# Attention in a fused encoder block: each transposition of probabilities as two halves of 64 queries

## What is computed

```
x = x + 1/2 * SwiGLU_1(RMSNorm(x))
h = RMSNorm(x);  q_r,k_r,v_r,g_r, q_a,k_a,v_a, gate_r,gate_a = h @ W_in
A: retention, 4 heads, both directions      B: windowed attention, see below
x = x + W_out( sigmoid(gate_r) * A + sigmoid(gate_a) * B )
x = x + 1/2 * SwiGLU_2(RMSNorm(x));  y = RMSNorm(x)
```

```
m = max(max(sc), sink);  p = exp(sc - m);  p = p / (sum(p) + exp(sink - m));  o = p @ v
```

## Time and profile before

| | us |
|---|---|
| median of 3 runs (2065.56 to 2068.51) | 2066.97 |
| the profiled execution | 2067.74 |
| its span in the trace | 2065.9 |
| TensorE busy, share of the span | 98% |
| VectorE, ScalarE, GpSimd | 64%, 35%, 44% |

### The profile page before, as it was taken

One profiled execution on the slowest core, in us unless ns is written; L12 is line 12 of the kernel. 1 busy time (PEld: TensorE's weight loads), 2 busy tenths in 40 slices (PEclk: granted clock), 3 DMA queues, 4 the chain that ended last, 5 costly groups with the idle time before them and its releaser, 6 DMA issues. The chain is left out here.

```text
span 2065.9 us, 25975 instructions
## 1 busy us (share of the span) xinstructions
PE 2018.8 (98%) x9240; PEld 1646.5 (80%) x9240; DVE 1328.3 (64%) x1478; ACT 731.6 (35%) x975; POOL 900.3 (44%) x564
## 2 busy tenths in 40 slices
PE   8999999999999999999999999999999999989997
PEld 7888888877877888888876668888888888877876
DVE  7766666677776525525676665467766666677765
ACT  5433333343333321222224554325333333343332
POOL 0244344478996312212122212252334334479992
PEclk8999999999999999999999999999999999999998
DMA  3232333366352211111211124331423323383532
GB/s 136 87 122 90 103 112 106 117 218 209 123 173 97 87 62 43 59 61 41 92 41 62 43 91 137 144 134 62 133 97 100 108 96 121 110 283 130 192 97 82
DMA packets 106865, 227.29 MB, mean 110 GB/s; under 512 B 9392, under 2 KB 30000, under 8 KB 106800
## 3 DMA queue, kind: packets, MB, share of 16 engines
q1 hardware_dynamic: 75680, 175.14, 24.9%
q10 hardware_dynamic: 31120, 51.29, 7.1%
HBM read 165.05 MB, written 61.34 MB: 110 GB/s over the span
## 5 line engine op out<-in xcount | busy, mean ns | idle before, releaser
L2042 POOL TENSOR_TENSOR w_lo<-stage,w_hi 128x1024 fp32r<-128x1024 f32 x54 | 143.0, 2649 | 437.2 <-ACT w_hi L1001 437.2
L1619 DVE SCALAR_TENSOR_TENSOR x<-ps,x 128x512 f32<-128x512 f32 x280 | 187.3, 685 | 106.4 <-PE ps L669 103.9
L600 PE MATMUL ps<-a_hi,w_hi 128*128 128x512 f32 x752 | 250.3, 400 | 1.1 <-DVE q_a L1810 0.6
L600 PE MATMUL ps<-a_lo,w_hi 128*128 128x512 f32 x752 | 242.9, 391 | 0.0
L600 PE MATMUL ps<-a_hi,w_lo 128*128 128x512 f32 x752 | 242.8, 391 | 0.0
L2057 POOL TENSOR_TENSOR gb<-gb,rstd 128x512 f32<-128x512 f32 x42 | 92.4, 2201 | 323.6 <-DVE gb L1551 301.9
L600 PEld LDWEIGHTS ps<-a_hi,w_hi 128*128 128x128 f32 x752 | 140.3, 188 | 37.4 <-issue 10.9
L600 PEld LDWEIGHTS ps<-a_hi,w_lo 128*128 128x128 f32 x752 | 141.5, 188 | 29.9
L600 PEld LDWEIGHTS ps<-a_lo,w_hi 128*128 128x128 f32 x752 | 141.8, 189 | 27.4
L669 PE MATMUL ps<-t_hi,hi 128*128 128x512 f32 x352 | 139.1, 395 | 13.0 <-DVE x L1619 8.1
L669 PE MATMUL ps<-t_lo,hi 128*128 128x512 f32 x352 | 137.3, 390 | 0.0
(11 more groups left out here) (309 smaller groups left out, 4606.9 us busy)
## 6 DMA issues: line engine op xcount, KB each, us to landing
stage<-wstream SPq DMA_DIRECT2D x56, 512.0 KB, 3.5
b_spill<-diff SPq DMA_DIRECT2D x88, 256.0 KB, 3.7
st_a<-win SPq DMA_DIRECT2D x42, 512.0 KB, 3.4
st_b<-win SPq DMA_DIRECT2D x42, 512.0 KB, 4.0
t_lo<-b_spill SPq DMA_DIRECT2D x40, 512.0 KB, 7.5
b_spill<-rawv SPq DMA_DIRECT2D x66, 256.0 KB, 4.0
a_lo<-b_spill SPq DMA_DIRECT2D x30, 512.0 KB, 5.1
x<-xT SPq DMA_DIRECT2D x16, 512.0 KB, 6.5
```

Source lines behind the costliest of these rows:

```text
L600: mm = pe.matmul(ps[:, bank, :], w[0:r, k, :], mv[0:r, k, HALF * half:HALF * half + HALF], start=first and part == 0, stop=final and part ...
L1619: dve.scalar_tensor_tensor(out=x[:, m, part], in0=ps[:, bank, :], scalar=0.5, in1=x[:, m, part], op0=ALU.mult, op1=ALU.add).then_inc(xacc, 1)
L2042: pool.tensor_tensor(w_lo[:, parity, :, :], stage[:, parity, :, :], f32(w_hi[:, parity, :, :]), ALU.subtract).then_inc(wlo_done, 1)
```

## The change

Each 128x128 transposition becomes two of 64 queries x 128 keys. The half with queries 0 to 63 lies in rows 0 to 63 of the array and goes to bank 6; the half with queries 64 to 127 lies in rows 64 to 127 and goes to bank 7. One `turn_p` so fills half of both banks, and every `turn_p` waits for the copy of the one directly before it. In the gate units the three calls of each half move from after k-steps 1, 2, 3 to after 1, 3, 5, and from after 0, 1, 2 to after 0, 2, 4. ScalarE's copy reads 256 numbers of each of two banks and puts the halves of each head together again.

```diff
                 else:
-                    pe.wait_ge(pT_done, 6 * i + (idx - 1 + SEED))
+                    pe.wait_ge(pT_done, 6 * i + (idx + SEED))
                 for a in range(GRP):
-                    mm = pe.transpose(ps[:, 6 + idx % 2, P * a:P * a + P], pr[kv][:, a, P * j:P * j + P], ident)
+                    for u in range(2):
+                        rows = slice(64 * u, 64 * u + 64)
+                        mm = pe.transpose(ps[:, 6 + u, 64 * a:64 * a + 64], pr[kv][rows, a, P * j:P * j + P], ident[rows, rows])
                 mm.then_inc(p_turned, 1)
...
-                    if before is not None and 1 <= k <= 3:
-                        turn_p(before, 1, k - 1)
+                    if before is not None and k in (1, 3, 5):
+                        turn_p(before, 1, k // 2)
...
-                      between=lambda k: turn_p(i, 0, k) if k <= 2 else None).then_inc(unit_done, 1)
+                      between=lambda k: turn_p(i, 0, k // 2) if k in (0, 2, 4) else None).then_inc(unit_done, 1)
...
-                    act.activation(pT[kv][:, j, :], ps[:, 6 + (3 * kv + j) % 2, :], ACT.Copy).then_inc(pT_done, 1)
+                    act.activation(pT[kv][:, j, :].rearrange("p (a u n) -> p u a n", a=GRP, u=2),
+                                   ps[:, 6:8, 0:256].rearrange("p u (a n) -> p u a n", a=GRP), ACT.Copy).then_inc(pT_done, 1)
```

## The result

The change made the kernel slower by 0.75%: 2084.01 us in the median of 4 runs (2082.22 to 2085.49) against 2066.26 (2062.97 to 2068.51), ratio 1.0075 with a 95% interval of 1.0058 to 1.0092. Forecast were 2080.4 and a ratio of 2080.4/2066.97 = 1.0065. The profiled execution has a span of 2080.8 us against 2065.9.

The account below looks back on a forecast made before the run. TensorE, busy 98% of the span and all of an attention block, was taken as the bound. Turns 6.3, score waits 6.0 and the tail after block 7 1.1 sum to 13.4 us, giving a median of 2080.4, range 2077 to 2085.

Parts of the forecast that it names:

- TensorE's stream decides: Attention block: TensorE is busy in all 19.75 us, so a longer turn_p lengthens the kernel.
- A turn costs 0.58 in place of 0.44: Each turn_p on TensorE: +0.14 us, 6.3 us over the 45 turns inside gate halves.
- the gap of 0.32: Entry of a turn: from last gate matmul to first half's load, 0.32 where 0.23 is seamless, costing 0.09 us.
- the exposed load: First weight load of a turn's halves, not hidden behind other work: 0.058 us.
- steps of 0.06: Inside a turn: row halves run side by side, leaving four steps of 0.058, together 0.23 us.
- the exit: From a turn back to gate matmuls: change of shape 0.09 and exposed load 0.11, together 0.20 us.
- The concurrency that I took from the scores: Halves of a transposition in different rows run side by side, as the scores' 64-row matmuls do.
- The rival with dearer pairs: Turns: loads of 0.107 or halves in turn cost +0.33 or +0.37 each, about 2090 us; chance 0.20.
- The scores wait 0.85 at seven places: Next block's first scores wait for exponentials behind the later third copy, blocks 1 to 7: 6.0 us.
- five covers (a) to (e): Waits that stay covered: turns for copies, values for third copy, second scores for exponentials, turn for p, exponentials for bias.
- After block 7 +1.1: Three turns in a row lose their second buffer, +0.7 us, and the first waits for p, +0.4 us.
- The sum: Whole kernel: 6.3 + 6.0 + 1.1 = 13.4 us, so 2081.1 for the profiled execution, 2080.4 for the median.

Follow-up runs that it names:

- e8: Changed kernel with both halves of every transposition taking queries 0 to 63, so all eight lie in rows 0 to 63; 2103.65 us in a single execution.
- e6: Kernel before, with the first two turns of each second half made as row halves directly behind the second scores, the third whole in bank 0; ratio 0.9991.
- e2_late_only: Kernel before, whole transpositions in alternating banks, with only the calls moved to after k-steps 1, 3, 5 and 0, 2, 4; ratio 1.0039.
- e1_split_early: Changed kernel with halves and their waits kept, but the calls back after k-steps 1, 2, 3 and 0, 1, 2; ratio 1.0042.
- e5_exps_first: Changed kernel, but ScalarE makes the exponentials of the second scores before the third copy of the second half; ratio 1.0044.
- e10_whole_at_end: Changed kernel, but the three turns behind block 7 are whole transpositions in alternating banks; 2084.43 us in a single execution.

## Why the prediction was right

**TensorE's stream decides.** Right: the whole change of the span lies in the attention stage, and the earlier trace rows gave no gap to hide in.

**A turn costs 0.58 in place of 0.44.** Right: 0.59 (0.585 to 0.60 in all but the first turn of block 0, which waits for p in both kernels). Its pieces hold one by one: the gap of 0.32, the exposed load (52 ns against 58 taken), steps of 0.06, the exit. The concurrency that I took from the scores is shown by e8 against the changed kernel, the cost of the changes of shape by e6: the same pairs behind the scores cost 0.25 a turn, inside the gate half 0.59. The rival with dearer pairs is out. It had rested in part on the Trainium skill ("TensorE: Matmul & The Clock Gate", section "LDWEIGHTS"), by which such a load takes 107 ns. The trace has 52, and the measurement decides.

**The scores wait 0.85 at seven places.** Right: 0.90 to the load and 0.93 to the first matmul, 6.5 us in all against 6.0. e2_late_only makes the wait by the places alone; e1_split_early and e5_exps_first take it away, one by the place and one by ScalarE's order. None of the five covers (a) to (e) broke.

**After block 7 +1.1.** The mechanism was right (0.4 for p and 0.8 for the rounds, of 1.16 each where 1.13 were forecast), the size was not: +2.8 with the fall of the clock, a term that the sum lacked. I had read the clock only in the stage as it was, and not asked what three rounds of 0.46 work and 0.69 waiting do to it.

**The sum.** Forecast 13.4, measured in the stage 16.4: turns 6.7 for 6.3, waits 6.5 for 6.0, after block 7 2.8 for 1.1, and 0.4 in gate matmuls between turns, which no term had. By the ratio of the runs it is 15.5 us (12 to 19), and 2084.01 lies at the upper end of the forecast's own range. That the profiled execution came as near as 2082.64 to the 2081.1 forecast for it is in part luck: the rest of the program was 1.5 us shorter in it.

## What to carry to other kernels

In this kernel matmuls in fewer rows saved time only beside others of their shape: each visit inside 128-row work cost 0.35 us for two changes of shape and two exposed weight loads, more than the 0.2 that half-size pieces could save, and the same pieces put directly behind work of their own shape gained 0.4 us for every two turns. When a call is moved later, look at what stands behind its result on the next engine, and count the work that is left to cover it: two k-steps fewer turned a slack of 0.35 us into a wait of 0.9. In a stage that is full on TensorE every such tenth of a microsecond came back as time, block after block.

## What the runs showed of the hardware that I had not expected

- Instructions in different groups of rows most likely pass each other. With four transpositions for rows 0 to 63 ahead of four for rows 64 to 127, the eight began two by two and took 0.47; with all eight in one group they began one by one and took 0.71. The Trainium skill's "TensorE: Matmul & The Clock Gate", section "Part 3: Packing small matmuls — row/col tiling", has matmuls start and end in program order; these two runs speak against that across groups of rows, unless the banks explain the difference.
- TensorE's granted clock fell to the lower level (0.53 granted over the next 3.6 us) within the attention stage behind a stretch of 3.4 us in which it was busy 1.39 us. It stayed at the upper level where TensorE was busy 2.30 of 3.4 us (e10_whole_at_end) and 2.32 of 4.0 us (e8_same_rows).
- Gate matmuls cost some 0.015 us more for each turn when turns stand two k-steps apart and not one (11.30 against 11.25 for three turns, between first matmuls of e2_late_only and of the kernel before). The cause is open.
